# Odd attention of a two-layer mixer: last gate store and first masks ahead of a weight panel, other buffers for the probabilities, output projection waiting bank by bank

## The chip, the cores and the metric

The kernel runs on one core of one Trainium2 chip, as one program written by hand for the engines TensorE (PE in the profile), VectorE (DVE), ScalarE (ACT), GpSimd (POOL) and SyncE (SP), which issues the DMAs. The metric is the device time of one execution in microseconds (us), taken as the median of the runs.

## The reference, cut to what matters

Three layers follow each other over 1024 positions of width 1024: an even layer (windowed attention and a state-space mixer), an odd layer (attention over keys picked by an indexer), and a second block. The change lies in the odd layer, whose core is:

```
q, k, v, gate, qi, ki, wi = split_cols(hn @ w_in, ODD_SPLITS)
q, k = rms_norm(q), rms_norm(k)                  # 8 heads of 128, 2 key/value heads
att = dsa_attention(q, k, v, qi, ki, wi, rel_bias)
return (att * jax.nn.silu(gate)) @ w_out         # h = h + this
```

In `dsa_attention` a query block of 128 positions sees the 256 keys of the highest index score: `logits = q.k / sqrt(Dh) + bias`, everything else is `NEG_INF`, then `softmax` and the product with `v`.

## The kernel before, in words

**Panels.** Every weight matrix comes as panels of at most 128 x 1024 values. SP loads panel i into one of two raw buffers (`sp_panel`, after the low part of panel i-2 has been made from that buffer), ACT rounds it to the high part (`act_panel`, line 297, "w_hi"), POOL subtracts for the low part (`pool_panel`, line 307, "w_lo"), and PE uses three products of high and low parts (line 262). Four panels can be resident.

**The odd layer.** The projection ends with the panels og0 to og7, the gates. For each of them PE makes two halves of 24 matmuls, ACT applies silu into `gev[m % 2]` (line 2382), and SP stores that buffer to DRAM (`gscr`, line 2495, event "og_out" m). Beside it VectorE picks the keys of each block into the mask `MK` (event "keep", lines 2178 to 2187). ACT and POOL convert panel og_m + 4 after gate m; for og7 that is the fourth panel of the output projection.

**The attention** walks over 64 units (n, b), head n and query block b; unit b has 128 (b + 1) keys. All engines write the walk out and pass semaphores, and each engine executes in its own order:

- SP loads one bias strip per head (`load_strip`, line 2480) and one gate per head (`load_gate`, line 2489).
- POOL, `s0` (line 2436): for b of 2 or more, strip plus mask into one of two buffers `bms`.
- PE, `s1`: the products q.k into one of two pairs of PSUM banks, for which the pair has to be free ("od_L" of the unit before the last).
- VectorE, `s1` (line 2235): products plus window into the buffer `pr[i % 3]`, with the row's extreme.
- ACT, `s1` (line 2390): the exponential in place, with the row sums.
- PE, `s2` (line 265): transposes of the probabilities, two units later; ACT (line 2399) or VectorE (line 2250) copies them out.
- After each four blocks `s3`: PE spreads the reciprocal sums and multiplies with the values into bank 3; VectorE scales by sum and gate (lines 2258 and 2261, event "od_g"), ACT takes the high part `MH` (line 443, "od_hi"), POOL the low part `ML` (line 2441, "od_lo"). Q is 0 for blocks 0 to 3 and 1 for blocks 4 to 7.

**The output projection** (`pe_out`, stage "oo") works on t (the first or second 512 positions) and h (the half of the columns). For t = 0, h = 0 it takes three panels one after the other, for each of them the four blocks b in banks 0 to 3, and the fourth panel block by block. VectorE adds the layer's input, which SP has loaded again from DRAM (line 2506), into the result (line 481).

Two buffers share memory with the gates: `gev` lies at H0 + 12 KB and H0 + 16 KB, and `pr` before lies at H0 + 16, 24 and 28 KB. So unit (0, 0) writes over the buffer from which gate 7 is stored, and waits:

```
if (n, b) == (0, 0):
    dve.wait_ge(*at("og_out", 7))
```

The output projection begins after `mixed(t)`, which waits for "od_hi" and "od_lo" of all heads of that t, and for the marks of all four engines at the end of the attention.

Of the kernel before, what the change touches and what calls it, by code (L numbers as in the profile page):

```python
# [17 lines left out]
KB = 1024  # L18
# [1789 lines left out]
class Odd:  # L1808


    def __init__(self, k, E):
        PH, H0, X0 = k.PH0, k.H0, k.X0
        self.XN = E.XN
        self.QT = k.tile(PH, [8, 1024])
        self.KT, self.VN = k.tile(PH + 32 * KB, [2, 1024]), k.tile(PH + 40 * KB, [8, 256])
        self.MK, self.TN = k.tile(PH + 48 * KB, [33 * 128], BF16), k.tile(PH + 48 * KB + 8448, [128])
        O = PH + 48 * KB + 8960
        self.sq = [k.tile(O + 2 * KB * i, [512]) for i in range(2)]
        self.mo = {b: sum(128 * (c + 1) for c in range(2, b)) for b in range(2, 9)}
        self.QI, self.KI = k.tile(H0, [4, 1024]), k.tile(H0 + 16 * KB, [1024])  # L1820
        self.SC = {7: k.tile(H0 + 24 * KB, [1024]), 6: k.tile(H0 + 28 * KB, [896]), 5: k.tile(O + 4 * KB, [768])}

        off = PH + 48 * KB + 2 * self.mo[5] - 768
        for b in (2, 3, 4):
            self.SC[b] = k.tile(off, [128 * (b + 1)])
            off += 512 * (b + 1)
        self.WIT = k.tile(H0 + 24 * KB, [1024])
        self.WI = k.tiny[:, 128:192].rearrange("p (b n) -> p b n", b=8)

        self.by_dve, self.by_act = [6, 4, 3, 2], [7, 5]  # L1830
        self.col = {b: i for i, b in enumerate((6, 4, 3, 2, 7, 5))}
        self.CNT, self.FEW, self.NEED = k.tiny[:, 64:70], k.tiny[:, 70:76], k.tiny[:, 108:114]
        self.TB, self.UB = k.tiny[:, 96:102].bitcast(I32), k.tiny[:, 102:108].bitcast(I32)
        self.ULP, self.BIG = k.tiny[:, 114:116], k.tiny[:, 116:118]
        self.EQ, self.PS = k.tile(H0, [1024]), k.tile(H0 + 4 * KB, [1024])
        at = {6: 0, 4: 1792, 3: 3072, 7: 4096, 5: 6144}
        self.JK = {b: k.tile(H0 + o, [128 * (b + 1)], BF16) for b, o in at.items()}
        self.JK[2] = k.tile(O + 7 * KB, [384], BF16)
        self.rs = k.tile(H0 + 8 * KB, [1024])
        self.gev = [k.tile(H0 + (12 + 4 * i) * KB, [1024]) for i in range(2)]  # L1840
        self.qg, self.ZS = k.tiny[:, 80:81], k.tiny[:, 192:211]
        self.x0 = Ring(k, "od_x0", [0, 1, 2, 3], [("h1", 0, b) for b in range(4, 8)])
        self.x1 = Ring(k, "od_x1", [4, 5, 6, 7], [("h1", 1, b) for b in range(4, 8)])
        self.proj = Ring(k, "od_proj", [0, 1, 2], [("free", "od_x0", "on_t", 0, 4 + i) for i in range(3)])

        self.held = ((3, ("free", "od_x0", "on_t", 0, 7)), (4, ("free", "od_x1", "on_t", 1, 4)))
        self.mis = Ring(k, "od_mis", [5, 6, 7], [("free", "od_x1", "on_t", 1, 5 + i) for i in range(3)])
        self.rel = Ring(k, "od_rel", [k.tile(H0 + 20 * KB + 2 * KB * i, [512]) for i in range(2)])
        self.order = [7, 6, 5, 4, 3, 2]

        self.chain = [("score", b, h) for b in self.order for h in range(8)]
        for i in range(32):
            self.chain += [("count", i, b) for b in self.by_dve + self.by_act] + [("bits", i)]

        done = [min(32, (29 * (u + 1)) // 20) for u in range(32)]
        self.deal = [7 * (b - a) for a, b in zip([0] + done, done)]

        self.norms = [(n, half) for n in (8, 0, 1, 2, 3, 4, 5, 6, 7, 9) for half in range(2)]

        self.bms = [k.tile(H0 + 4 * KB * i, [1024]) for i in range(2)]  # L1860
        self.strips = [k.tile(H0 + o * KB, [1024]) for o in (20, 8)]
        self.pr = [k.tile(H0 + o * KB, [1024]) for o in (16, 24, 28)]
        self.pts = [k.tile(X0, [4, 4, 128]), k.tile(X0 + 8 * KB, [8, 4, 128])]
        self.gts = [k.tile(X0 + (24 + 4 * i) * KB, [1024]) for i in range(2)]
        self.MH, self.ML = k.tile(PH, [8, 1024], F32R), k.tile(X0 + 32 * KB, [8, 1024], F32R)
        self.smr = [k.tiny[:, 128 + 8 * i:136 + 8 * i] for i in range(3)]

        self.sums, self.recs = ([k.tiny[:, o + 4 * i:o + 4 * i + 4] for i in range(2)] for o in (152, 160))
        self.pairs = [4, 6]
        self.ptb = Ring(k, "od_ptb", [0, 1, 2], [("free", "od_proj", "og", *use) for use in ((7, 1), (6, 1), (7, 0))])  # L1870
        self.units = [(n, b) for n in range(8) for b in range(8)]
        self.emb = [k.tile(PH + (48 + 4 * q) * KB, [1024]) for q in range(3)]
# [35 lines left out]
def tensor_odd(k, O):  # L1908
# [143 lines left out]
            s2(*O.units[i - 2])  # L2052
    k.mark("od_att")

    def mixed(t):
        for n in range(8):
            pe.wait_ge(*at("od_hi", n, t))
            pe.wait_ge(*at("od_lo", n, t))
        k.marks(pe, "od_att")

    pieces = [((O.MH, O.ML), 2 * i, 0) for i in range(4)]
    pe_out(k, "oo", lambda t: pieces, lambda t, h, b: [("h2", h, b - 4)] if t else [], mixed,
           lambda part: pe_transposes(k, k.second.x0, "xs", lambda b: k.H[:, b, :], lambda b: [("ln0_y", b)], (0,), range(4 * part, 4 * part + 4)))
    k.mark("odd")


def vector_odd(k, O):
# [152 lines left out]
    def s1(n, b):  # L2220
        nk, i = 128 * (b + 1), 8 * n + b
        p, sm = O.pr[i % 3][:, 0:nk], O.smr[i % 3]
        three = before((n, b), 3)
        if three:
            dve.wait_ge(*at("od_P_turned", *three))
        if b >= 2:
            win = O.bms[b % 2][:, 0:nk]
            dve.wait_ge(*at("od_bm", n, b))
        else:
            win = O.strips[n % 2][:, 1024 - nk:1024]  # L2230
            dve.wait_ge(*at("od_strip", n))
        dve.wait_ge(*at("od_S", n, b))
        if (n, b) == (0, 0):
            dve.wait_ge(*at("og_out", 7))
        V.tensor_tensor_reduce(out=p, in0=k.bank(O.pairs[b % 2], 2)[:, 0:nk], in1=win, scale=-1.0, scalar=3e38,  # L2235
                               op0=ALU.add, op1=ALU.min, accum_out=sm[:, 0:1]).then_inc(*up("od_L", n, b))

# [181 lines left out]
def pool_odd(k, O):  # L2419
    pool, nc, at, up, last = k.pool, k.nc, k.at, k.up, k.last  # L2420
    G = nc.gpsimd
    pool.wait_ge(*at("on_t_ps", 1, 7))
    k.marks(pool, "even")
    G.memset(O.TN, 0.0).then_inc(*up("causal", 0))
    pool.wait_ge(*last("causal"))
    G.affine_select(out=O.TN, in_=O.TN, compare_op=ALU.is_ge, fill=-3e38, base=0, pattern=[[-1, 128]], channel_multiplier=1).then_inc(*up("causal"))
    for name in ("qi0", "qi1", "qi2", "qi3", "ki", "ok0", "ok1", "ov0", "ov1", *(f"oq{m}" for m in range(8)), *(f"og{m}" for m in range(8))):
        pool_panel(k, PANEL_AT[name] + 4)
    def s0(n, b):
        if b >= 2:  # L2430
            nk = 128 * (b + 1)
            pool.wait_ge(*at("od_strip", n))
            pool.wait_ge(*at("keep", 7))
            if (n, b) not in ((0, 2), (0, 3)):
                pool.wait_ge(*at("od_L", *((n, b - 2) if b >= 4 else (n - 1, b + 4))))
            G.tensor_tensor(O.bms[b % 2][:, 0:nk], O.strips[n % 2][:, 1024 - nk:1024], O.MK[:, O.mo[b]:O.mo[b] + nk], ALU.add).then_inc(*up("od_bm", n, b))  # L2436

    def s3(n, Q):
        o = slice(512 * Q, 512 * Q + 512)
        pool.wait_ge(*at("od_hi", n, Q))  # L2440
        G.tensor_tensor(O.ML[:, n, o], O.gts[n % 2][:, o], O.MH[:, n, o].bitcast(F32), ALU.subtract).then_inc(*up("od_lo", n, Q))  # L2441

    s0(*O.units[0])
    for i in range(len(O.units) + 4):
        if i + 1 < len(O.units):
            s0(*O.units[i + 1])
        if i >= 4 and O.units[i - 4][1] % 4 == 3:
            s3(O.units[i - 4][0], O.units[i - 4][1] // 4)
    k.mark("od_att")
    pool_out(k, "oo", "ln0", lambda: k.marks(pool, "od_att"))  # L2450
    k.mark("odd")


def sync_odd(k, O):
# [35 lines left out]

    load_strip(0)
    for m in range(8):
        sp_panel(k, PANEL_AT[f"og{m}"] + 6)
        sp.wait_ge(*at("og", m, 1))
        S.dma_start(d["gscr"][128 * m:128 * m + 128], O.gev[m % 2]).then_inc(*up(f"og_out{m % 2}", by=16, also=[("og_out", m)]))
    sp.wait_ge(*at("og_ps", 7, 1))
    load_gate(0)
    load_strip(1)
    for n, b in O.units:
        if 0 < n < 7 and b == 0:  # L2500
            load_strip(n + 1)
# [1261 lines left out]
```

## Time and profile before

| | |
|---|---|
| median of 3 runs | 2109.1 us (2109.01 to 2120.7) |
| the profiled execution, its own time | 2109.57 us |
| its span in the profile | 2108.3 us |
| mean granted TensorE clock | 0.988 of full |
| PE busy | 2022.3 us, 96% of the span |
| DVE, ACT, POOL busy | 1410.3, 873.4, 653.2 us |

A row of the timeline gives start, duration, engine, line, operation, and output and inputs with the buffer numbers left out; instructions of one kind are merged, and the bracket says how long the engine sat idle before and what released it. The busy share of PE is the share of time in which matmuls are under way. The granted clock is 1.00 at 2.4 GHz and 0.50 at 1.2 GHz; a window that holds a change of level shows a value between.

### The profile page before, as it was taken

How to read it: one execution, taken by the hardware profiler on the slowest of the kernel's cores; microseconds unless marked ns; L12 is line 12 of the kernel's file. 1: busy time of each engine (PE TensorE's matmuls, PEld its weight loads, DVE VectorE, ACT ScalarE, POOL GpSimd, SP SyncE). 2: the span in 40 equal slices, each digit the busy share in tenths (PEclk: the TensorE clock that was granted, in tenths of full speed). 3: DMA queues.
4: the chain of work that ended last, by engine and by line, in shares of the span. 5: the costliest groups of instructions: out<-in, count | busy, mean ns of one | idle time of the engine just before them, and what ended most of it. 6: DMA issues, size and time to landing. Idle time of an engine off the chain costs nothing.

```text
span 2108.3 us, 24436 instructions
## 1 busy us (share of the span) xinstructions
PE 2022.3 (96%) x9260; PEld 1536.7 (73%) x9260; DVE 1410.3 (67%) x2159; ACT 873.4 (41%) x1524; POOL 653.2 (31%) x484
## 2 busy tenths in 40 slices
PE   8999989999999999899999999999999989999997
PEld 6778856787557676566678787888787667778885
DVE  7668676422346889445517699899998756784649
ACT  5333276333445662344412333444224544362431
POOL 3676520552101112345434000000003544235443
PEclk9999999999999999999999999999999999999999
DMA  6422330442401112311043211121133112556322
GB/s 259 134 58 77 109 118 21 170 140 76 135 20 41 41 51 80 100 41 50 21 170 114 86 42 60 32 79 50 60 110 117 64 55 73 193 190 219 110 81 110
DMA packets 72429, 197.91 MB, mean 94 GB/s; under 512 B 11182, under 2 KB 20559, under 8 KB 71800
## 3 DMA queue, kind: packets, MB, share of 16 engines
q1 hardware_dynamic: 72168, 196.35, 27.2%
q8 instruction: 73, 1.20, 0.2%
q14 instruction: 44, 0.36, 0.1%
q10 hardware_dynamic: 144, 0.00, 0.0%
HBM read 152.89 MB, written 46.71 MB: 95 GB/s over the span
## 4 chain that ended last, share of the span: by engine, by line
PE 60%; DVE 16%; ACT 4%; issue 3%; POOL 2%; DMA 2%; SPq 0%; DVEq 0%; ACTq 0%; POOLq 0%
PE psum L262 57%; DVE m L2878 3%; PE psum L265 3%; POOL m L307 1%; DMA m<-in_w 1%; DVE m L2899 1%; DVE m L2111 1%; PE psum L1984 1%; ACT m L297 1%; DVE m L317 1%; DVE m L536 1%; DVE m L452 1%; DVE m L527 1%; DVE m L3070 1%; DVE m L3051 1%
## 5 line engine op out<-in xcount | busy, mean ns | idle before, releaser
L262 PE MATMUL psum<-m,m 128*128 128x512 f32 (+8 forms) x8420 | 1920.8, 393 | 51.9 <-DVE m L2235 10.6
L262 PEld LDWEIGHTS psum<-m,m 128*128 128x128 f32 (+4 forms) x8420 | 1443.0, 187 | 503.3 <-issue 157.6
L307 POOL TENSOR_TENSOR m<-m,m 128x1024 fp32r<-128x1024 f32 (+1 forms) x122 | 309.0, 2537 | 1023.1 <-ACT m L297 1022.7
L297 ACT ACTIVATE m<-m 128x1024 fp32r<-128x1024 f32 (+2 forms) x166 | 173.6, 1049 | 355.0 <-PE psum L262 222.7
L2878 DVE SCALAR_TENSOR_TENSOR m<-m,m,m 128x1024 f32<-128x1024 f32 x240 | 310.2, 1294 | 6.3
L265 PE MATMUL psum<-m,m 128*128 128x128 f32 x784 | 110.5, 277 | 20.3 <-ACT m L2399 5.7
L265 PEld LDWEIGHTS psum<-m,m 128*128 128x128 f32 x784 | 90.5, 142 | 40.8 <-ACT m L1431 10.6
L2111 DVE TENSOR_SCALAR_CACHE_REDUCE m<-m,m 128x896 bf16<-128x896 f32 (+4 forms) x130 | 102.7, 847 | 1.0
L2235 DVE CUSTOM_DVE_ANT_0 m<-psum,m 128x128 f32<-128x128 f32 (+3 forms) x64 | 48.2, 754 | 55.2 <-POOL m L2436 21.5
L2436 POOL TENSOR_TENSOR m<-m,m 128x384 f32<-128x384 f32 (+5 forms) x48 | 72.2, 1525 | 11.3 <-DVE m L2235 11.3
L2341 ACT ACTIVATE m<-m,m 128x1024 bf16<-128x1024 f32 (+1 forms) x62 | 64.1, 1037 | 23.6 <-DVE m L2138 23.6
L2390 ACT ACTIVATE m<-m,m 128x128 f32<-128x128 f32 (+3 forms) x64 | 49.6, 774 | 55.8 <-DVE m L2235 55.8
L2090 DVE SCALAR_TENSOR_TENSOR m<-m,m,m 128x512 f32<-128x512 f32 (+1 forms) x70 | 43.7, 656 | 41.7 <-ACT m L2325 40.1
L317 DVE TENSOR_TENSOR m<-m,m 128x1024 fp32r<-128x1024 f32 (+1 forms) x44 | 52.7, 1198 | 24.6 <-ACT m L297 24.5
L481 DVE TENSOR_TENSOR m<-psum,m 128x512 f32<-128x512 f32 x32 | 21.3, 684 | 66.4 <-PE psum L262 59.9
L443 ACT ACTIVATE m<-m 128x512 fp32r<-128x512 f32 (+1 forms) x38 | 33.5, 883 | 60.6 <-DVE m L2261 52.8
L2325 ACT ACTIVATE m<-psum 128x512 f32<-128x512 f32 (+1 forms) x80 | 38.7, 522 | 42.7 <-PE psum L262 32.1
L465 POOL TENSOR_TENSOR m<-m,m 128x1 f32<-128x1 f32 x23 | 31.5, 1372 | 58.6 <-DVE m L458 58.6
L2441 POOL TENSOR_TENSOR m<-m,m 128x512 fp32r<-128x512 f32 x16 | 20.4, 1274 | 88.4 <-ACT m L443 88.4
L2899 DVE SCALAR_TENSOR_TENSOR m<-m,m,m 128x1024 f32<-128x1024 f32 x36 | 46.2, 1283 | 0.9
L2956 DVE TENSOR_TENSOR m<-m,m 128x1024 f32<-128x1024 f32 x16 | 20.6, 1290 | 38.4 <-ACT m L3233 38.4
L402 DVE SCALAR_TENSOR_TENSOR m<-psum,m,m 128x512 fp32r<-128x512 f32 x32 | 21.6, 743 | 31.3 <-ACT m L391 31.3
(305 smaller groups left out, 1649.4 us busy)
## 6 DMA issues: line engine op xcount, KB each, us to landing
m<-in_w SPq DMA_DIRECT2D x164, 512.0 KB, 3.5
scr_hscr<-m SPq DMA_DIRECT2D x4, 2048.0 KB, 6.6
m<-scr_hscr SPq DMA_DIRECT2D x4, 2048.0 KB, 10.9
scr_turned<-scr_strip SPq DMA_DIRECT2D x8, 575.5 KB, 12.6
m<-in_x SPq DMA_DIRECT2D x4, 1024.0 KB, 7.8
scr_gscr<-m SPq DMA_DIRECT2D x16, 256.0 KB, 4.1
m<-in_x SPq DMA_DIRECT2D x2, 2048.0 KB, 8.4
m<-scr_turned SPq DMA_DIRECT2D x8, 512.0 KB, 3.5
```

Of the source, the lines that this page charges most:

```text
L262: return self.nc.tensor.matmul(out, lhsT, rhs, start=start, stop=stop, skip_group_check=True)
L265: return self.nc.tensor.transpose(out, in_, self.ident[:, :])
L297: k.nc.scalar.activation(k.hi[SLOT[i]][:, 0:kk * n], k.raw[i % 2][:, 0:kk * n], ACT.Copy).then_inc(*k.up("w_hi", i))
L307: k.nc.gpsimd.tensor_tensor(lo, raw, hi.bitcast(F32), ALU.subtract).then_inc(*k.up("w_lo", i))
L317: k.nc.vector.tensor_tensor(lo, raw, hi.bitcast(F32), ALU.subtract).then_inc(*k.up("w_lo", i))
L2111: V.tensor_scalar(O.JK[b], O.SC[b], TF[:, c:c + 1] if i else 0.0, None, how, ALU.add, accum_out=CNT[:, c:c + 1]).then_inc(*up("count", i, b))
L2235: V.tensor_tensor_reduce(out=p, in0=k.bank(O.pairs[b % 2], 2)[:, 0:nk], in1=win, scale=-1.0, scalar=3e38, op0=ALU.add, op1=ALU.min, accum_ ...
L2341: A.activation(O.JK[b], O.SC[b], ACT.Sign, bias=O.TB.bitcast(F32)[:, c:c + 1] if i else 0.0, accum_out=O.CNT[:, c:c + 1]).then_inc(*up("si ...
L2390: A.activation(p, p, ACT.Exp, bias=sm[:, 0:1], scale=-1.0, accum_out=O.sums[b // 4][:, b % 4:b % 4 + 1]).then_inc(*up("od_exp", n, b))
L2436: G.tensor_tensor(O.bms[b % 2][:, 0:nk], O.strips[n % 2][:, 1024 - nk:1024], O.MK[:, O.mo[b]:O.mo[b] + nk], ALU.add).then_inc(*up("od_bm", ...
L2878: V.scalar_tensor_tensor(o, u[:, j:j + 1024], w[:, j:j + 1], o, ALU.mult, ALU.add).then_inc(*up("cv_tap", m, j))
L2899: V.scalar_tensor_tensor(o, x[:, j:j + 1024], cw[:, j:j + 1], o, ALU.mult, ALU.add).then_inc(*up("xb_tap", i, j))
```

## The change

- SP stores the last gate before it loads the weight panel og7 + 6, not behind it; the second strip and the first gate are fetched before that panel too.
- POOL makes the masks of units (0, 2) and (0, 3) before it converts the panel og7 + 4, not behind it.
- The buffers `pr` are at H0 + 24, 28 and 12 KB in place of 16, 24 and 28 KB. Unit (0, 0) waits for no store; unit (0, 2), whose buffer is that of gate 6, waits for "og_out" 6.
- The output projection waits for each bank and each pair of heads where it first uses them, in place of all marks and all heads ahead of its first matmul. SP's own wait for the marks ahead of the reload of the layer's input stays.

```diff
-        self.pr = [k.tile(H0 + o * KB, [1024]) for o in (16, 24, 28)]
+        self.pr = [k.tile(H0 + o * KB, [1024]) for o in (24, 28, 12)]
...
-    def mixed(t):
-        for n in range(8):
+    def free(t, h, b):
+
+        if t:
+            return [("h2", h, b - 4)]
+        if h:
+            return [("od_L", 7, 6 + b // 2)]
+        return [("free", "od_ptb", *O.ptb.holder[b])] if b < 3 else [("od_g", 7, 1)]
+
+    def ready(t, h, i):
+        for n in (2 * i, 2 * i + 1):
             pe.wait_ge(*at("od_hi", n, t))
             pe.wait_ge(*at("od_lo", n, t))
-        k.marks(pe, "od_att")
...
-        if (n, b) == (0, 0):
-            dve.wait_ge(*at("og_out", 7))
+        if (n, b) == (0, 2):
+            dve.wait_ge(*at("og_out", 6))
...
-    for name in ("qi0", "qi1", "qi2", "qi3", "ki", "ok0", "ok1", "ov0", "ov1", *(f"oq{m}" for m in range(8)), *(f"og{m}" for m in range(8))):
+    panels = ["qi0", "qi1", "qi2", "qi3", "ki", "ok0", "ok1", "ov0", "ov1", *(f"oq{m}" for m in range(8)), *(f"og{m}" for m in range(8))]
+    for name in panels[:-1]:
         pool_panel(k, PANEL_AT[name] + 4)
...
-    s0(*O.units[0])
+    for i in range(4):
+        s0(*O.units[i])
+    pool_panel(k, PANEL_AT[panels[-1]] + 4)
     for i in range(len(O.units) + 4):
-        if i + 1 < len(O.units):
+        if 4 <= i + 1 < len(O.units):
             s0(*O.units[i + 1])
...
     for m in range(8):
-        sp_panel(k, PANEL_AT[f"og{m}"] + 6)
+        if m < 7:
+            sp_panel(k, PANEL_AT[f"og{m}"] + 6)
         sp.wait_ge(*at("og", m, 1))
         S.dma_start(d["gscr"][128 * m:128 * m + 128], O.gev[m % 2]).then_inc(*up(f"og_out{m % 2}", by=16, also=[("og_out", m)]))
+    load_strip(1)
     sp.wait_ge(*at("og_ps", 7, 1))
     load_gate(0)
-    load_strip(1)
+    sp_panel(k, PANEL_AT["og7"] + 6)
```

On POOL, where the projection ends and the attention begins, the order before is this (m_62, m_66 and m_70 are the raw, high and low buffers of the panel, m_183 and m_184 the two `bms`, m_185 the strip, m_157 the mask):

```order
L307 TENSOR_TENSOR m_69<-m_63,m_65 128x1024 [waits act_w]
L307 TENSOR_TENSOR m_70<-m_62,m_66 128x1024 [waits act_w]
L2436 TENSOR_TENSOR m_183<-m_185,m_157 128x384 [waits dve_idx,od_strip0]
L2436 TENSOR_TENSOR m_184<-m_185,m_157 128x512
L2436 TENSOR_TENSOR m_183<-m_185,m_157 128x640 [waits dve_od]
```

And with the change, on the same engine at the same place:

```order
L307 TENSOR_TENSOR m_69<-m_63,m_65 128x1024 [waits act_w]
L2445 TENSOR_TENSOR m_183<-m_185,m_157 128x384 [waits dve_idx,od_strip0]
L2445 TENSOR_TENSOR m_184<-m_185,m_157 128x512
L307 TENSOR_TENSOR m_70<-m_62,m_66 128x1024 [waits act_w]
L2445 TENSOR_TENSOR m_183<-m_185,m_157 128x640 [waits dve_od]
```

The two masks of 384 and 512 columns have moved ahead of the last panel's low part; the third mask stays behind it.

On VectorE, the first units of the attention before (m_187 to m_189 are the three `pr`, and out4 is the semaphore of the store of gate 7, out0 that of gate 6; each unit has a second instruction that reads the accumulator):

```order
L2235 ISA m_187,m_59<-psum,m_185 128x128 [waits out4,pe_od,od_strip0]
L2235 ISA m_59 128x1
L2235 ISA m_188,m_59<-psum,m_185 128x256 [waits pe_od]
L2235 ISA m_59 128x1
L2235 ISA m_189,m_59<-psum,m_183 128x384 [waits pe_od,pool_od]
```

And with the change:

```order
L2242 ISA m_187,m_59<-psum,m_185 128x128 [waits pe_od,od_strip0]
L2242 ISA m_59 128x1
L2242 ISA m_188,m_59<-psum,m_185 128x256 [waits pe_od]
L2242 ISA m_59 128x1
L2242 ISA m_189,m_59<-psum,m_183 128x384 [waits out0,pe_od,pool_od]
```

The wait for a store has moved from the first unit to the third, and is for the store of the gate before.

On PE, the first matmuls of the output projection, in one piece of the difference (m_67 and m_71 hold the high and low part of a panel, m_194 and m_195 are `MH` and `ML`):

```order
-L262 MATMUL psum<-m_67,m_194 128x512 [waits pool_od,pe_od,act_od,dve_od,act_w,pool_w]
+L262 MATMUL psum<-m_67,m_194 128x512 [waits act_w,dve_od,pool_w,pool_od]
 L262 MATMUL psum<-m_71,m_194 128x512
 L262 MATMUL psum<-m_67,m_195 128x512
```

The order of the matmuls is the same; the first one waits for earlier events of VectorE and POOL, and for none of ACT, and the nineteenth (block 3, "od_g") has a wait for VectorE of its own.

## Rows read from the trace of the kernel before

**Rows 1.** The page: busy time, share of the span and instructions of each engine.

```profile
PE 2022.3 (96%) x9260; PEld 1536.7 (73%) x9260; DVE 1410.3 (67%) x2159; ACT 873.4 (41%) x1524; POOL 653.2 (31%) x484
```

**Rows 2.** Waits of PE over the run: total, times, longest.

```profile
PE psum L262 <- DVE m L2235: 10.6, 8, 9.5
```

**Rows 3.** Timeline, 855 to 877 us: start us, us, engine, line, operation.

```profile
855.08 0.69 DVE L2187 TENSOR_SCALAR m<-m 128x1024 bf16<-128x1024 f32 x1
...
855.47 11.83 PE L262 MATMUL psum<-m,m 128*128 128x512 f32 x52
...
867.17 1.05 ACT L297 ACTIVATE m<-m 128x1024 fp32r<-128x1024 f32 x1
868.24 1.28 ACT L2390 ACT_TABLE_LOAD   x1
868.30 2.34 POOL L307 TENSOR_TENSOR m<-m,m 128x1024 fp32r<-128x1024 f32 x1 [10.26 <-ACT m L297]
870.59 2.02 POOL L2436 TENSOR_TENSOR m<-m,m 128x384 f32<-128x384 f32 x2
...
871.09 0.42 SPq L2495 DMA_DIRECT2D scr_gscr<-m  x1
...
876.41 0.29 DVE L2235 CUSTOM_DVE_ANT_0 m<-psum,m 128x128 f32<-128x128 f32 x1 [19.32 <-DMA scr_gscr<-m]
...
876.74 0.40 ACT L2390 ACTIVATE m<-m,m 128x128 f32<-128x128 f32 x1 [7.22 <-DVE m L2235]
...
876.76 1.65 PE L262 MATMUL psum<-m,m 128*128 128x384 f32 x2 [9.47 <-DVE m L2235]
```

**Rows 4.** Source line 2495, the store of a gate: issue to landing.

```profile
DMA to landing us min/median/max: 4.9/5.0/5.1
```

**Rows 5.** PE by window: window, length, busy (matmuls), granted clock, DMA share, GB/s.

```profile
871.00:872.00 1.00, 0.00 (x0) 0.79 0.50 57
...
881.00:882.00 1.00, 1.00 (x2) 0.59 0.00 0
```

**Rows 6.** Timeline: POOL's third mask, unit (0, 4).

```profile
879.20 1.40 POOL L2436 TENSOR_TENSOR m<-m,m 128x640 f32<-128x640 f32 x1 [6.59 <-DVE m L2235]
```

**Rows 7.** Timeline, 1052 to 1063 us: end of the attention.

```profile
1052.43 7.05 PE L262 MATMUL psum<-m,m 128*128 128x128 f32 x24
...
1059.59 0.69 DVE L2261 TENSOR_TENSOR m<-psum,m 128x512 f32<-128x512 f32 x1 [5.33 <-PE psum L262]
...
1061.02 1.26 POOL L2441 TENSOR_TENSOR m<-m,m 128x512 fp32r<-128x512 f32 x1 [9.03 <-ACT m L443]
...
1062.67 22.61 PE L262 MATMUL psum<-m,m 128*128 128x512 f32 x90 [3.19 <-POOL m L2441]
```

**Rows 8.** PE in windows of 1 us at the output projection's beginning.

```profile
1062.00:1063.00 1.00, 0.33 (x1) 0.86 0.00 0
...
1066.00:1067.00 1.00, 1.00 (x5) 0.93 1.08 438
```

**Rows 9.** PE in windows of 1 us at another short idle stretch.

```profile
544.00:545.00 1.00, 0.00 (x0) 1.00 0.00 0
...
547.00:548.00 1.00, 1.00 (x5) 0.66 1.00 295
```

**Rows 10.** Timeline: first addition of the layer's input, and the seventh panel's low part.

```profile
1082.54 0.69 DVE L481 TENSOR_TENSOR m<-psum,m 128x512 f32<-128x512 f32 x1 [22.26 <-PE psum L262]
...
1083.24 2.40 POOL L307 TENSOR_TENSOR m<-m,m 128x1024 fp32r<-128x1024 f32 x1 [3.76 <-ACT m L297]
```

**Rows 11.** Source line 2506, two reloads of the layer's input: issue to landing.

```profile
DMA to landing us min/median/max: 7.7/10.8/13.9
```

**Rows 12.** Waits of PE from 1085 to 1200 us.

```profile
PE psum L262 <- issue: 1.8, 1, 1.8
```

**Rows 13.** Timeline of ACT, 1161 to 1163 us: a table load and what follows.

```profile
1161.04 1.28 ACT L3166 ACT_TABLE_LOAD   x1 [2.17 <-DMA scr_hscr<-m]
1162.33 0.69 ACT L3166 ACTIVATE m<-psum,m 128x512 f32<-128x512 f32 x1
```

More of the change, by code:

```diff
@@ L2053, in tensor_odd @@
     k.mark("od_att")
-    def mixed(t):
-        for n in range(8):
+    def free(t, h, b):
[6 more added lines that the diff above has]
+        for n in (2 * i, 2 * i + 1):
             pe.wait_ge(*at("od_hi", n, t))
             pe.wait_ge(*at("od_lo", n, t))
-        k.marks(pe, "od_att")
     pieces = [((O.MH, O.ML), 2 * i, 0) for i in range(4)]
-    pe_out(k, "oo", lambda t: pieces, lambda t, h, b: [("h2", h, b - 4)] if t else [], mixed,
-           lambda part: pe_transposes(k, k.second.x0, "xs", lambda b: k.H[:, b, :], lambda b: [("ln0_y", b)], (0,), range(4 * part, 4 * part + 4)))
+    pe_out(k, "oo", lambda t: pieces, free, lambda t: None,
+           lambda part: pe_transposes(k, k.second.x0, "xs", lambda b: k.H[:, b, :], lambda b: [("ln0_y", b)], (0,), range(4 * part, 4 * part + 4)), 2, ready)
     k.mark("odd")
```

## The prediction

> **What bounds the kernel now.** I began with the page's busy shares: PE has matmuls under way in 96% of the span [rows 1], so only time in which PE stands still or runs at the lower clock can be won; a shorter wait on another engine is worth something only if PE waits behind it. The list of PE's waits came next. Its largest entry, 10.6 us, is a wait for VectorE's line 2235, and one single wait makes 9.5 us of it [rows 2]. The timeline around that wait shows the end of the gate projection and the start of the attention [rows 3], and the same view at the attention's end shows the second place that the change touches [rows 7]. The windows of 1 us then say at which clock PE ran after each [rows 5, 8].
>
> At the first place PE ends its 52 matmuls (48 of gate 7, four of the first two units) at 855.47 + 11.83 = 867.30 us and resumes at 876.76: 9.47 us idle. VectorE had been idle for 19.32 us and started at 876.41, released by the store of the gates. That store was issued at 871.09, behind the load of a weight panel which waited for POOL's low part (868.30 to 870.64), and took about 5 us [rows 3, 4]: 871.09 + 5.1 = 876.2. At the second place PE ends at 1059.48, and the chain VectorE (1059.59), ACT, POOL (until 1062.28) ends before it resumes at 1062.67: 3.19 us idle [rows 7].
>
> **The first wait.** Unit (0, 0) no longer writes into gate 7's buffer, so VectorE starts when PE's first product is there. Before, PE followed 876.76 - 876.41 = 0.35 us after VectorE's start [rows 3]; the same step from 867.3 puts PE's next product at about 867.65. Removed: 9.47 us. New: 0.35 us. Unit (0, 2) waits for the store of gate 6 instead. No row shows that store by itself; stores are issued after ACT's silu of their gate and land after about 5 us [rows 4], and gate 7 alone occupied PE for 48 of the 52 matmuls of an 11.83 us row, so it is long over when the buffer is needed. I cost it at nothing; if the cover were gone, it would be a part of the 5 us.
>
> **The clock behind it.** The granted clock stood at 1.00 until 871.6 us (0.79 in the window from 871) and came back at 881.8 (0.59 in the window from 881) [rows 5]; so from 876.76 to 881.8 PE worked at 1.2 GHz. 5.06 us at half the clock are worth up to 2.5 us where PE sets the pace. In this stretch the engines also hand small units to each other, so the value lies between 0 and 2.5; I take 2.5 here and subtract the new waits singly.
>
> **What is late next: ScalarE's exponential.** The code of ACT is not changed. After gate 7 it copies a panel (867.17 to 868.22), loads the table for the exponential (868.24 to 869.52), and only then can treat unit (0, 0); before, all of this was hidden behind the store, and the exponential came at 876.74, 0.33 us after VectorE's start [rows 3]. Now PE has the product of unit (0, 2) to do, from 867.65, which took 1.65 us at the lower clock [rows 3] and so about 0.8 at the higher, until 868.5; then come the transposes of unit (0, 0), for which the exponential must be done: 869.52 + 0.40 plus a hand-over like the 0.35 above is 870.3. PE waits 1.8 us there. So the bottleneck of the first units becomes ACT's queue, and 0.35 + 1.8 = 2.15 us of the 9.47 remain.
>
> A load of another table followed at once by its activation is in the trace: 1161.04 + 1.28 = 1162.32, and the activation begins at 1162.33 [rows 13]; also, the load at 868.24 begins 0.02 us after the copy before it. The Trainium skill, page "ScalarE: Activation LUTs", section "What ACT_TABLE_LOAD costs", gives 1283 ns for the load and about 1380 ns more of drain for every switch. The first number agrees with the rows, the second is not seen in them. By that rule the exponential would come about 1.4 us later and the sum below would be 1.4 us smaller, an estimate from that page.
>
> **Masks and POOL.** The masks of (0, 2) and (0, 3) take 2.02 us together [rows 3]. POOL sat idle for 10.26 us before 868.30 [rows 3], and the last pass over the mask ends at 855.08 + 0.69 = 855.8 [rows 3], so both fit into the idle stretch and are ready at about 860. They cost nothing, and without this step VectorE would have waited for them until 872.6. The converted panel stays at 868.30 to 870.64, since it waits for ACT. The third mask comes behind it: from 870.64 for 1.40 us [rows 6], thus 8.6 us earlier than its old start at 879.20. POOL thus permits a gain of 8.6 us here plus what slack the mask had; I see it as a bound near the sum, not below it. The panel is the fourth of the output projection, 190 us away.
>
> **SP's queue.** The gate store moves from 871.09 to about 867.7, the strip of head 1 and the gate of head 0 go out behind it, then the panel, whose condition (POOL's low part at 870.64) is not changed. Each issue is a fraction of a microsecond, and the three transfers of half a megabyte land between about 873 and 878; the first gate is needed at the first `s3`, which stands behind eight units' worth of PE's order. Nothing is gained or lost.
>
> **A new spell of low clock.** A fall of the clock can follow rather short idle times: around 544 us PE had one window of 1 us without a matmul, and at 547.7 the clock fell [rows 9]. The spell at the output projection lasted from 1062.72 to 1066.14, 3.42 us [rows 8]. The 2.15 us that remain can bring one like it, at 0 to 1.7 us; I take 0.9.
>
> First place: 9.47 + 2.5 - 2.15 - 0.9 = 8.9 us.
>
> **The second wait.** PE needs for its first matmul the panel (resident), bank 0 (released by VectorE's scaling before the last product), and heads 0 and 1 of the first 512 positions. None of these depends on the last block, whose part ends at 1062.28; that is used only for t = 1, after all of t = 0. Bank 3 is read by VectorE from 1059.59 for 0.69 us, until 1060.28. With the new wait PE comes to it after three blocks of six matmuls. 90 matmuls took 22.61 us [rows 7], 0.25 each, so that is 4.5 us after 1059.5, at 1064: covered by 3.7 us. The whole 3.19 us go, less a hand-over that I put at 0.1.
>
> With the idle stretch the spell from 1062.72 to 1066.14 goes as well: 3.42 x 0.5 = 1.7 us, between 0 (it comes all the same) and 1.7. It is the only idle time of that length near, so I take the whole.
>
> Second place: 3.19 - 0.1 + 1.7 = 4.8 us.
>
> **What follows.** From 1085 to 1200 us PE waits once, 1.8 us, for nothing that the profile shows [rows 12]; the work behind follows PE. SP still waits for all marks ahead of the reload of the layer's input, so relative to the projection the reload becomes 4.8 us later. It lands 7.7 us (first half) and 13.9 us (second) after the issue [rows 11], just behind 1062.3, so by 1070 and 1076.7. VectorE first needs it at 1082.54, now 1077.7: covered by 7 us. The seventh panel's low part ends at 1083.24 + 2.40 = 1085.6 [rows 10]; PE, which uses four panels for the first 22.6 us, comes to the seventh at about 1062.67 + 6 x 5.7 = 1096.9, now 1092: covered by 6 us.
>
> **The sum.** 8.9 + 4.8 = 13.7 us. The profiled execution took 2109.57 us, so 2095.9. The median shown is 2109.1, 0.5 below that execution; I predict 2095.4 us.
>
> **Rivals.**
>
> *The start gains less* (ACT stays behind through several units, a drain behind the table load, POOL's conversion slower beside VectorE). 9.47 + 2.5 - 2.15 - 1.7 - 1.4 = 6.7, and without any value for the old spell 4.2. With 4.8 that is 9.0 to 11.5: 2097.6 to 2100.1. For it speaks that five engines hand over small units there. Against it, that each part alone is small.
>
> *The projection gains nothing*: PE stands again at its first new wait, for instance bank 0 or a panel. Then 8.9 alone, 2100.2. Nothing in the rows supports it.
>
> *More than the sum*: no new spell of low clock (+0.9), and a spell later in the run that falls away because the phases shift, 1.7 us each: 2091 to 2094. To be faster by over 1% (below 2088.0) it would take 21 us; the removable parts, 9.47 + 2.5 + 3.19 + 1.7, are 16.9.
>
> *Slower than before*: the output projection starts while the reload of the input and the weights share the DMA queue, and the addition of the input waits. The price is one microsecond of VectorE, and then of PE through the banks, for each microsecond of landing beyond the 7 us of cover. To lose the 13.7 us too, the first reload would have to land more than 28 us after its issue, where 7.7 and 13.9 are measured.
>
> *The change does not do what it says*: a wait of another name at the same time, such as the strip or a count of stores; 2109. The order shows none.
>
> **How the numbers follow.** The sum as argued, 2093 to 2097.5: 0.67. Start gains less: 0.15. Projection gains nothing: 0.05. More than the sum: 0.09, with 0.03 beyond 1%. Slower or unchanged: 0.04, half of it beyond 1%. A measurement of this kernel can tell about 1% (21 us) from no change, so the gain lies inside "within 1%": faster 0.03, same 0.95, slower 0.02. The range for 8 in 10 goes from 2091.5, where a later spell also falls away, to 2100.5, which takes in the weaker start.
>
> **What would show it.** PE's idle time between gate 7 and unit (0, 2) is 0.3 to 0.5 us, followed by one near 1.8 us that ends with ACT's line 2390 (a few lines lower in the new file). The two first masks stand at 858 to 860 us, ahead of POOL's last panel. The store of gate 7 is issued near 867.7. The clock in the windows from 871 to 881 is 1.00, or has at most one spell of 3.4 us. PE has no idle time between the last product with the values and the projection, and no fall of the clock behind. The prediction fails if PE waits in the first units for POOL's masks, if the clock falls for longer than one spell, or if a new wait appears on weight panels after 1080.

## The result, and the profile after

Twenty runs of each: the changed kernel 2101.9 us median (2095.1 to 2110.3), the kernel before 2113.1 us (2107.6 to 2121.2). The ratio is 0.9941, interval 0.9929 to 0.9954, so 12.5 us less of 2113 (9.7 to 15.0); the two medians differ by 11.2 us. I had forecast 13.7 us less, which lies in that interval, and 2095.4 us, which is wrong: the range ended at 2100.5. The median of the three runs shown of before, 2109.1, was low for this kernel: of the twenty, only two others are as short or shorter, and the comparisons with other runs of it below give 2112.6 (a single run) to 2115.6.

The timeline of the changed kernel, at the beginning of the attention (columns as in [rows 3]):

```profile
859.10 0.69 DVE L2194 TENSOR_SCALAR m<-m 128x1024 bf16<-128x1024 f32 x1
...
859.48 12.81 PE L262 MATMUL psum<-m,m 128*128 128x512 f32 x54
...
862.01 2.04 POOL L2445 TENSOR_TENSOR m<-m,m 128x384 f32<-128x384 f32 x2
...
871.02 0.29 DVE L2242 CUSTOM_DVE_ANT_0 m<-psum,m 128x128 f32<-128x128 f32 x1 [9.92 <-PE psum L262]
871.19 1.05 ACT L297 ACTIVATE m<-m 128x1024 fp32r<-128x1024 f32 x1
...
872.25 1.28 ACT L2397 ACT_TABLE_LOAD   x1
872.31 2.34 POOL L307 TENSOR_TENSOR m<-m,m 128x1024 fp32r<-128x1024 f32 x1 [8.26 <-ACT m L297]
...
873.55 0.40 ACT L2397 ACTIVATE m<-m,m 128x128 f32<-128x128 f32 x1
...
874.10 0.33 PE L265 MATMUL psum<-m,m 128*128 128x128 f32 x1 [1.81 <-ACT m L2397]
874.26 1.02 PE L262 MATMUL psum<-m,m 128*128 128x512 f32 x2
...
875.34 1.25 PE L262 MATMUL psum<-m,m 128*128 128x512 f32 x4
```

These answer to [rows 3]. VectorE starts when PE's product is there, not when a store has landed. The products of unit (0, 2) are merged into PE's row of 54, so the 0.35 us ahead of them is not even shown as idle. The masks (862.01) lie ahead of POOL's panel (872.31). What is late is ScalarE: copy, table load, and 0.02 us behind the load the first exponential; PE stands still for 1.81 us.

At the attention's end, the same view (answers to [rows 7]):

```profile
1046.59 28.76 PE L262 MATMUL psum<-m,m 128*128 128x128 f32 x117
...
1053.75 0.69 DVE L2268 TENSOR_TENSOR m<-psum,m 128x512 f32<-128x512 f32 x1 [5.34 <-PE psum L262]
...
1055.18 1.29 POOL L2450 TENSOR_TENSOR m<-m,m 128x512 fp32r<-128x512 f32 x1 [9.02 <-ACT m L443]
...
1071.88 0.69 DVE L481 TENSOR_TENSOR m<-psum,m 128x512 f32<-128x512 f32 x1 [17.44 <-PE psum L262]
```

The last products with the values and the projection are one row of 117 matmuls: PE doesn't stop while VectorE, ACT and POOL finish the last block. In windows of 1 us (window, length, busy, granted clock, DMA share, GB/s) the clock holds through both places:

```profile
872.00:873.00 1.00, 0.29 (x1) 1.00 0.90 356
873.00:874.00 1.00, 0.00 (x0) 1.00 1.08 242
874.00:875.00 1.00, 0.90 (x3) 1.00 0.96 328
...
1057.00:1058.00 1.00, 1.00 (x6) 1.00 0.46 53
```

**Two stretches as a measure.** An execution differs from the next by several microseconds, so I read two stretches in every trace: from the start of PE's row of gate 7 to VectorE's unit (0, 5) (the row with 128x768), and from there to the first addition of the layer's input (first row of line 481). Unit (0, 5) in the timeline before:

```profile
884.22 0.96 DVE L2235 CUSTOM_DVE_ANT_0 m<-psum,m 128x768 f32<-128x768 f32 x1 [0.70 <-PE psum L262]
```

And after:

```profile
878.38 0.96 DVE L2242 CUSTOM_DVE_ANT_0 m<-psum,m 128x768 f32<-128x768 f32 x1 [0.70 <-PE psum L262]
```

Before, 884.22 - 855.47 = 28.75 us and 1082.54 - 884.22 = 198.32 us (the other two ends are in [rows 3, 10]); after, 878.38 - 859.48 = 18.90 us and 1071.88 - 878.38 = 193.50 us. That is 9.85 + 4.82 = 14.67 us gained. Ahead of gate 7 and behind the addition the code is the same, but gate 7 begins 4.01 us later (859.48, not 855.47), and from the addition to the end of the span it takes 2100.3 - 1071.88 = 1028.4 us, where before it took 2108.3 - 1082.54 = 1025.8. The experiments had to say which of these two differences belong to the change.

### The profile page after: what moved, and what is told of

Same layout as the page of the kernel before. It is cut to its first block, busy times and chain, and to the rows that moved or that the text cites. A ratio compares the mean times of both kernels' runs of the same rounds, so it can differ in the third digit from the quotient of the medians.

```text
span 2100.3 us, 24435 instructions
## 1 busy us (share of the span) xinstructions
PE 2024.0 (96%) x9260; PEld 1538.4 (73%) x9260; DVE 1414.3 (67%) x2159; ACT 873.4 (42%) x1524; POOL 652.2 (31%) x484
## 4 chain that ended last, share of the span: by engine, by line
PE 64%; DVE 14%; ACT 5%; issue 2%; POOL 2%; DMA 1%; SPq 0%; DVEq 0%; ACTq 0%
PE psum L262 60%; PE psum L265 3%; DVE m L2891 2%; POOL m L307 1%; DMA m<-in_w 1%; DVE m L2912 1%; PE psum L1984 1%; DVE m L2118 1%; DVE m L536 1%; ACT m L297 1%; DVE m L452 1%; DVE m L527 1%; DVE m L3083 1%; ACT m L391 1%; DVE m L3064 1%
## 5 line engine op out<-in xcount | busy, mean ns | idle before, releaser
L2450 POOL TENSOR_TENSOR m<-m,m 128x512 fp32r<-128x512 f32 x16 | 20.4, 1275 | 88.3 <-ACT m L443 88.3
```

## The experiments

**Each place alone.** front_only has all of the change but the waits of the projection; end_only has only these, of which this is the core:

```diff
+        return [("free", "od_ptb", *O.ptb.holder[b])] if b < 3 else [("od_g", 7, 1)]
+
+    def ready(t, h, i):
+        for n in (2 * i, 2 * i + 1):
             pe.wait_ge(*at("od_hi", n, t))
             pe.wait_ge(*at("od_lo", n, t))
-        k.marks(pe, "od_att")
```

> Only the beginning of the attention is changed (buffers, first masks, order of SP's issues); the output projection waits as before. Theory A (the two places add, and what is measured elsewhere is the TensorE clock falling at other places by chance): from the start of PE's row of gate 7 to VectorE's unit (0, 5) 18.9 us as in the changed kernel (28.75 before), from there to the first addition of the layer's input 198.3 us as before; time 9.8 us below before, a ratio near 0.9953. Theory B (a shift by the first place brings falls of the clock further down that are there each time, and a part is given back): the same two stretches, but a gain of 5 to 8 us and falls of the clock at about the same later places in each profile of a shifted kernel, near 1220 and 1308 us.

> Only the waits of the output projection are changed; the beginning of the attention is as before. Theory A: from gate 7 to unit (0, 5) 28.75 us, from there to the first addition of the layer's input 193.5 us, 4.8 less than before, of which 3.2 are idle time and 1.6 the clock that does not fall; time 4.8 us below before, ratio near 0.9977. Theory B: the same stretches, but the gain does not show in the time. A further rival: the idle stretch goes and the clock falls all the same, then 195.1 us and a ratio near 0.9985.

front_only: 18.90 and 198.32 us, ratio 0.9951 (0.9934 to 0.9968). end_only: 28.85 and 193.36 us, ratio 0.9981 (0.9968 to 0.9994). The two places add, in the traces to 0.1 us and in time (0.9951 x 0.9981 = 0.9932) within the interval. In end_only the wait and the fall of the clock behind it go together.

**What the order of SP's issues is worth alone.** store_wait_kept:

```diff
-        self.pr = [k.tile(H0 + o * KB, [1024]) for o in (24, 28, 12)]
+        self.pr = [k.tile(H0 + o * KB, [1024]) for o in (16, 24, 28)]
...
-        if (n, b) == (0, 2):
-            dve.wait_ge(*at("og_out", 6))
+        if (n, b) == (0, 0):
+            dve.wait_ge(*at("og_out", 7))
```

> The changed kernel with the old buffers for the probabilities and the old wait of unit (0, 0) for the store of gate 7; the store is still issued ahead of the panel. The store goes out 0.4 us after the silu of gate 7 and takes 5.1 us, so VectorE starts 12.7 + 5.3 = 17 us or a little more after the start of the gate 7 row, 3.5 us earlier than before. Theory A: PE idles 5.7 to 6 us in place of 9.5 and of the changed kernel's 0.4 + 1.8; the exponential no longer has PE wait for its table; from gate 7 to unit (0, 5) 24 to 25.5 us, with a fall of the clock. Rival: if the order of the issues is the whole gain, 19 to 20 us.

21.90 us: less than I expected, more than the rival. The timeline shows why:

```profile
865.81 0.33 SPq L2507 DMA_DIRECT2D scr_gscr<-m  x1
...
868.85 0.29 DVE L2242 CUSTOM_DVE_ANT_0 m<-psum,m 128x128 f32<-128x128 f32 x1 [13.25 <-DMA scr_gscr<-m]
...
869.21 0.91 PE L262 MATMUL psum<-m,m 128*128 128x384 f32 x2 [3.40 <-DVE m L2242]
```

VectorE, which waits for the store, starts 3.0 us after it is issued, so the store took at most that, not 5. In [rows 3, 4], and for gate 6 in this trace, a panel load of the same size goes out 0.4 us ahead of the store; here nothing does, and only the next strip follows 0.4 us behind it. That this is the reason rests on one store, and the view of source line 2507 lists no landing as short (4.9 to 5.1 us). PE waits 3.40 us, the exponential finds its table loaded, and the low clock lasts 3.4 us in place of 10.2. So the order of the issues alone brings 6.85 of the 9.85 us, and the other buffers 3.0.

**The masks.** masks_behind:

```diff
+    pool_panel(k, PANEL_AT[panels[-1]] + 4)
     for i in range(4):
         s0(*O.units[i])
-    pool_panel(k, PANEL_AT[panels[-1]] + 4)
```

> The changed kernel with POOL's first two masks behind the last panel's low part again. POOL's panel ends 15.2 us after the start of the gate 7 row and the mask of (0, 2) takes 0.9 us more, so VectorE has unit (0, 2) at 16.1 and (0, 3) at 17.2 us in place of 12.9 and 16.0. Theory A: from gate 7 to unit (0, 5) 20 to 20.6 us, 1.1 to 1.7 more than the changed kernel, since ScalarE's table load hides the rest. Rival (the moved masks carry the gain): 22 us or more.

21.46 us, 2.56 more than the changed kernel, between my figure and the rival's:

```profile
870.79 2.34 POOL L307 TENSOR_TENSOR m<-m,m 128x1024 fp32r<-128x1024 f32 x1 [10.26 <-ACT m L297]
...
873.08 4.99 POOL L2445 TENSOR_TENSOR m<-m,m 128x384 f32<-128x384 f32 x4
...
874.04 0.56 DVE L2242 CUSTOM_DVE_ANT_0 m<-psum,m 128x384 f32<-128x384 f32 x1 [3.78 <-POOL m L2445]
...
874.66 2.50 PE L262 MATMUL psum<-m,m 128*128 128x512 f32 x4 [0.68 <-DVE m L2242]
```

VectorE waits 3.78 us for the mask, as expected, and PE 0.68 us more; but here the clock falls for 3.4 us (from 874 us on), and the row of four matmuls takes 2.50 us where the changed kernel's takes 1.25 (the row at 875.34 above). I had left that price out.

**The clock as a price of its own.** filled_wait is the kernel before with work in the place of PE's wait:

```diff
     for i in range(len(O.units) + 4):
+        if i == 2:
+            pe.wait_ge(*at("head_ms", 0))
+            for _ in range(10):
+                k.mm(k.bank(3)[:, 0:512], O.QT[:, 0, 0:128], O.KT[:, 0, 0:512], True, True)
```

> The kernel before, with ten extra products of 128 x 512 by TensorE into bank 3 ahead of unit (0, 2), whose result nothing reads: about 9.4 us of matmuls in the 9.47 us in which TensorE stood still. Theory A (the low clock behind the wait is a price of its own, up to 2.5 us): no fall of the clock from 871 to 882 us of the trace before, and from gate 7 to unit (0, 5) 26.2 to 27 us in place of 28.75. Rival (the small units set the pace there, whatever the clock): 28.5 us or more.

26.16 us, with VectorE's first unit at 20.83 us (20.94 before). The wait is as long as ever and the 2.6 us are the clock's. PE's rows:

```profile
861.92 20.41 PE L262 MATMUL psum<-m,m 128*128 128x512 f32 x72
883.10 0.91 PE L262 MATMUL psum<-m,m 128*128 128x384 f32 x2 [0.77 <-DVE m L2239]
```

0.91 us for the products of unit (0, 2), against 1.65 in [rows 3].

**The remaining 1.8 us.** exp_first, on the changed kernel:

```diff
-        act_panel(k, PANEL_AT[f"og{m}"] + 4)
+        if m < 7:
+            act_panel(k, PANEL_AT[f"og{m}"] + 4)
...
         if i < len(O.units):
             s1(*O.units[i])
+        if i == 7:
+            act_panel(k, PANEL_AT["og7"] + 4)
...
-    pool_panel(k, PANEL_AT[panels[-1]] + 4)
     for i in range(len(O.units) + 4):
         if 4 <= i + 1 < len(O.units):
             s0(*O.units[i + 1])
+        if i + 1 == 7:
+            pool_panel(k, PANEL_AT[panels[-1]] + 4)
```

> The changed kernel with the copy of the last panel of the projection moved on ScalarE behind the exponential of unit (0, 7), and its low part on POOL behind the mask of (0, 6). The table load then follows gate 7's silu at once, 1.05 us earlier. Theory A: PE's wait for the exponential of unit (0, 0) shrinks from 1.8 to about 0.75 us, and from gate 7 to unit (0, 5) 17.9 us in place of 18.9; from there to the first addition of the layer's input 193.4 us as before it. In time 1 us below the changed kernel, which a comparison of runs can't tell. Rival (the panel's move costs as much on POOL or SP, since the raw buffer and the next panel come later): the first stretch is 17.9 but the second longer than 193.4, or PE waits for a panel in the projection.

17.96 and 193.40 us, PE's wait 0.9 us: 0.94 us gained, with no cost in the second stretch. In time 0.9925 (0.9908 to 0.9941), beside after_again on the same chip at 0.9930: not told apart. Its two stretches together are the shortest of all traces, but the times do not show it to be faster.

**The same kernels again.**

> The changed kernel once more, nothing edited. Theory A (the level of a single execution is set by where the clock falls in code that the change does not touch): again 18.9 and 193.5 us in the two stretches to 0.2 us, while gate 7 begins at another time than 859.48 us, anywhere from 853 to 863, later where more spells of low clock lie ahead of it; ratio 0.993 to 0.995. Theory B (the change brings the later falls near 1220 and 1308 us): they are there again at those places.

> The kernel before once more, nothing edited. Theory A (where the clock falls outside the two places differs from one execution to the next): 28.75 and 198.3 us in the two stretches, gate 7 beginning anywhere from 853 to 863 us, and falls of the clock beyond 1190 us that need not be those of the first profile. Theory B (the falls near 1220 and 1308 us come with the change): none near 1220 to 1235 or 1308 to 1325 us here either, as in the first profile of the kernel before.

> A second repetition of the kernel before on the same chip. Theory A: again 28.75 and 198.3 us, and a start of gate 7 that differs from the repetition ahead of it by about half of the difference in time spent at the lower clock before it, when TensorE was at work. Theory B: no fall of the clock near 1220 to 1235 or 1308 to 1325 us.

after_again: 18.89 and 193.52 us, ratio 0.9930 (0.9911 to 0.9948). before_again_a: 28.82 and 198.31. before_again_b: 28.91 and 198.32. The two stretches repeat to 0.2 us, the start of gate 7 doesn't. All traces, with the time at the lower clock ahead of gate 7 added up from windows of 1 us:

```
                   gate 7   low clock  1st+2nd   addition  addition  low clock near (us of its own trace)
                   begins   before it  stretch   to 3051   to end    1187    1215-38   1304-22
before             855.47   13.6       227.07    776.0     1025.8    yes     no        no
before_again_a     861.16   27.2       227.13    776.2     1026.3    yes     no        no
before_again_b     856.38   17.0       227.23    776.2     1026.5    yes     no        no
filled_wait        861.92   30.6       224.59    776.7     1025.4    yes     no        no
before_fill_first  859.67   23.8       227.37    776.5     1025.3    no      yes       no
after              859.48   23.8       212.40    778.5     1028.4    no      yes       yes
after_again        862.38   30.6       212.41    777.7     1027.9    no      no        yes
front_only         862.35   27.2       217.22    777.3     1028.0    no      no        yes
end_only           862.21   30.6       222.21    777.8     1027.8    no      yes       yes
store_wait_kept    853.97   10.2       215.25    777.8     1028.5    no      yes       yes
masks_behind       857.95   20.4       214.82    778.5     1028.4    no      yes       no
exp_first          854.52   10.2       211.36    777.9     1028.2    no      yes       yes
after_fill_second  859.69   23.8       212.39    777.7     1026.5    no      no        yes
```

The column "to 3051" ends at VectorE's first instruction of line 3051, which is this row before:

```profile
1858.58 1.23 DVE L3051 TENSOR_TENSOR m<-m,m 128x1024 f32<-128x1024 f32 x1 [0.18 <-ACT m L3310]
```

And this one after:

```profile
1850.43 1.23 DVE L3064 TENSOR_TENSOR m<-m,m 128x1024 f32<-128x1024 f32 x1 [0.18 <-ACT m L3323]
```

First: up to gate 7 the work is the same in all of these, and it takes 853.97 to 862.38 us, in step with the time at the lower clock (20.4 us more of it, 7.4 to 8.4 us later). The 4.01 us by which gate 7 began later in the changed kernel's first trace are this: before_fill_first, whose code up to there is the kernel before, begins it at 859.67 with the same 23.8 us. Most of the spread of the runs goes with it too: of the twenty of the changed kernel, the two at a mean clock of 0.984 took 2108.47 and 2110.26 us and are the slowest, the five at 0.991 took 2095.12 to 2098.3. Theory A holds for that part.

Second: theory A is wrong behind the addition. Leave out the last two experiments (before_fill_first and after_fill_second, below). Seven traces with a part of the change take 1027.8 to 1028.5 us there, four without take 1025.4 to 1026.5. The means are 1028.2 and 1026.0: **2.2 us are given back** in the traces. 14.7 - 2.2 = 12.5 is the measured gain, but the interval of 9.7 to 15.0 us holds 14.7 as well, so the times by themselves do not show the 2.2.

**Where the 2.2 us go.** I followed ScalarE's sixteen activations of its line 3166 (3179 after) through both traces. The changed kernel is 10.66 us ahead at the addition, 10.12 at 1162, still 10.11 at 1401, and 8.32 at 1420 (times of the trace before). The twelfth and thirteenth of them before:

```profile
1401.05 0.69 ACT L3166 ACTIVATE m<-psum,m 128x512 f32<-128x512 f32 x1
...
1420.25 0.69 ACT L3166 ACTIVATE m<-psum,m 128x512 f32<-128x512 f32 x1 [2.61 <-PE psum L262]
```

And after:

```profile
1390.94 0.69 ACT L3179 ACTIVATE m<-psum,m 128x512 f32<-128x512 f32 x1
...
1411.93 0.69 ACT L3179 ACTIVATE m<-psum,m 128x512 f32<-128x512 f32 x1 [2.62 <-PE psum L262]
```

The 0.54 us ahead of 1162 are lost in filled_wait and before_fill_first too, so they are not the change's. Up to 1401 us the falls of the clock near 1220 and 1310 cost nothing in the end, and by 1420, where ScalarE waits for TensorE, they show. I take VectorE's taps (the multiply-adds of the second block's convolution, line 2878) for what sets the pace until about 1400; that is argued, no run shows it. The list of PE's waits in this part, for the kernel before (beside the wait of [rows 12]):

```profile
PE psum L265 <- ACT m L3146: 0.9, 1, 0.9
```

And for the changed kernel:

```profile
PE psum L265 <- ACT m L3159: 2.6, 1, 2.6
PE psum L262 <- issue: 1.8, 1, 1.8
```

Behind the same wait of 1.8 us the clock falls before and does not after; so PE arrives 1.6 us earlier at the next wait, which becomes longer by that much. I took this for the cause of the later falls and tried it from both sides, with products whose results nothing reads: before_fill_first puts seven into the wait of 1.8 us of the kernel before, after_fill_second eight into the wait of 2.6 us of the changed kernel. In both, TensorE's wait for the other engines is also moved behind its wait for a free bank, so that the products can stand between the two.

```diff
-            pe.wait_ge(*at("xs_hi", 1, 7))
-            pe.wait_ge(*at("xs_lo", 1, 7))
...
+        if (what, i, half) == ("gate", 0, 1):
+            for _ in range(7):
+                k.mm(bank, k.XH[:, 0, 0:128], k.XH[:, 0, 0:512], True, True)
+            pe.wait_ge(*at("xs_hi", 1, 7))
+            pe.wait_ge(*at("xs_lo", 1, 7))
```

The second:

```diff
-        pe.wait_ge(*at("xb_silu", i))
+        if i != 9:
+            pe.wait_ge(*at("xb_silu", i))
...
+            if i == 9 and half == 0:
+                for _ in range(8):
+                    k.mm(bank, k.XH[:, 0, 0:128], k.XH[:, 0, 0:512], True, True)
+                pe.wait_ge(*at("xb_silu", i))
```

> The kernel before, with seven extra products of 128 x 512 (about 1.7 us) by TensorE in the 1.78 us in which it waits near 1183 us, at the second block's first panel; nothing reads them. In four traces without a part of the change the clock falls behind this wait (1185 to 1191 us), in seven with a part of it not. Theory B' (the fall there is absorbed, since VectorE sets the pace until about 1400 us, and its absence sends TensorE into a longer wait near 1230 us and to falls near 1230 and 1320 us that are not absorbed): no fall near 1187, TensorE's wait for ScalarE near 1230 us 2.6 us in place of 0.9, and from the first addition of the layer's input to the end of the span 1027.5 to 1028.5 us in place of 1025.4 to 1026.5. Rival (the 2.2 us belong to something else in the change): still 1025.4 to 1026.5 us.

> The changed kernel, with eight extra products of 128 x 512 (1.9 us) by TensorE in its wait of 2.6 us for ScalarE near 1220 us; nothing reads them. Theory B' in its simple form (the long wait brings the falls behind it): no falls near 1220 and 1310 us, and from the first addition of the layer's input to the end 1025.5 to 1026.5 us in place of 1027.8 to 1028.5, so 2 us below the changed kernel, ratio near 0.993 or less. Rival (the fall near 1310 has another origin, as it follows no wait): it is there again and the stretch stays at 1027.8 or more.

before_fill_first: the fall near 1187 is gone, PE's wait is 2.5 us, the clock falls behind it (1238), and yet addition to end takes 1025.3 us: the rival. Only 0.26 us are lost between 1401 and 1420. after_fill_second: no fall near 1220, the one at 1309 is there again, and addition to end takes 1026.5; ratio 0.9931 (0.9908 to 0.9955), not told from the changed kernel. So my account in its simple form falls.

The total of after_fill_second still misleads. At line 3051, more than 400 us behind these places, all thirteen traces stand in two groups that do not overlap: 776.0 to 776.7 us from the addition without the change, 777.3 to 778.5 with a part of it, and after_fill_second is in the second with 777.7. The groups are 1.6 us apart in the mean; this part of what is given back shows in every trace. From there to the end the three kernels with added products (filled_wait and the last two) take 248.7 to 248.8 us and the ten others 249.7 to 250.8, with or without the change. This microsecond lies far behind the filled waits, TensorE's wait for VectorE's line 3017 is 2.3 to 2.4 us in them and 2.7 to 3.3 in the others, and the cause is open. It brings after_fill_second down to 1026.5, and without filled_wait the 2.2 us would be 2.0.

What the traces bear out is a price for each fall, which I read between ScalarE's rows at 1401 and 1420: the one near 1310 alone goes with 1.2 to 1.3 us lost (after_again, front_only, after_fill_second), the one near 1220 alone with 0.26 (before_fill_first, masks_behind), both together with 1.7 to 1.8 (after, end_only, store_wait_kept, exp_first). In masks_behind the rest goes with other falls, at 1492 and 1642. These prices are read off side by side; no run took the fall near 1310 away. Why the fall near 1310 comes in seven of eight traces with a part of the change and in none of five without stays open; it follows no wait that the profile shows:

```profile
1309.00:1310.00 1.00, 1.00 (x7) 1.00 0.00 0
1310.00:1311.00 1.00, 1.00 (x5) 0.84 0.00 0
1311.00:1312.00 1.00, 1.00 (x4) 0.50 0.00 0
```

## Why the prediction was right or wrong

- **The wait for the store** (9.47 us gone, 0.35 and 1.8 new): right. PE's new wait was 1.81 us and for ScalarE's exponential, as worked out.
- **The clock behind it** (up to 2.5, taken whole): right; filled_wait gave 28.75 - 26.16 = 2.59, of which 0.11 is an earlier start.
- **A new spell of low clock** (0.9 set aside): it did not come. With it left out the first place is 9.8 by my terms and 9.85 in the trace; I had 8.9. masks_behind shows that it was a real risk, one further wait away.
- **The drain of the table load** by the Trainium skill, page "ScalarE: Activation LUTs", section "What ACT_TABLE_LOAD costs": not seen. The exponential begins 0.02 us after the load.
- **The masks**: free in their new place, as argued; behind the panel they cost 2.56 us. "VectorE would have waited for them until 872.6" is when both masks end; unit (0, 2) needs the first alone, and in masks_behind VectorE has it 16.09 us after gate 7 begins, which is 871.6 in the trace before.
- **The store's 5 us**: at most 3.0 us in the one case without a panel load right ahead of it. The changed kernel doesn't depend on it.
- **The second wait** (3.19, less 0.1, and 1.7 for the clock): 4.82 measured against 4.8. The reload of the layer's input does not hold up the first addition, which is released by PE.
- **"The work behind follows PE"**: this step failed. I took it from a list of waits that ends at 1200 us. Behind it about 2 us are given back. Two errors partly cancelled here: I set 0.9 us aside at the first place for nothing and counted nothing for what is given back. That 13.7 us came near the measured 12.5 is in part luck.
- **The starting time, and the range**: the step that made the forecast wrong. "The median shown is 2109.1, 0.5 below that execution; I predict 2095.4 us" took three runs as the time of the kernel before, and twenty gave 2113.1. Of the 6.5 us between 2095.4 and 2101.9, 4.0 are this and 2.5 are the change's (13.7 against 11.2 between the medians). The trace had 13.6 us at the lower clock ahead of gate 7, other executions of the same code 10 to 31. With 2113.1 the same sum gives 2099.4, and the range moved by the same 4.0 would be 2095.5 to 2104.5, which holds the measured time. The range was built from the terms alone and held nothing for the spread of runs, though one of the three shown stood 11.6 us above the others.
- **A reading**: the fall that I put at 547.7 us in [rows 9] was at 547.3 (0.66 is about a third of the window at 1.00 and the rest at 0.50). No term of the sum used it.

Of the rivals, "the start gains less" and "the projection gains nothing" did not occur. "More than the sum" had the later falls of the clock vary, but only to the good side; they went to the other.

## What to carry to other kernels

Ahead of a phase change, write down for each engine what is queued there and in which order: here a store behind a panel load, two masks behind another, and an exponential behind a copy, and each was worth 1 to 7 us at one place. An idle stretch of TensorE cost its length and, at both places before, a spell of low clock as well (at the wait of 1.81 us after, none); both are in the windows, and a fill of the wait prices the second alone. When several executions differ by more than the change is worth, forecast the difference, take the time of the kernel before from many runs, and measure stretches between two named rows, which repeated here to 0.2 us for one kernel. Read the experiment's effect close to its place too: the three kernels with added products were 1 us shorter in a stretch hundreds of microseconds behind them.

## What the runs showed of the hardware that I had not expected

- The granted clock falls at places that differ from one execution to the next with the same code: 10.2 to 30.6 us at the lower level within the first 860 us, and with it gate 7 begins up to 8.4 us later. Behind one and the same wait of 1.8 us it fell in four of four traces and, with another part of the kernel changed far ahead of it, in none of eight. Another fall, near 1310 us, follows no wait at all, with TensorE at work in every window around it.
- A fall of the clock on TensorE can stay without effect and be paid much later: those at 1221 and 1310 us of the changed kernel's trace had cost 0.0 us at ScalarE's row of 1390.94 and 1.8 us at that of 1411.93.
- A store of half a megabyte, issued 0.4 us behind a load of the same size, landed after 5.0 us; the one store with nothing issued right ahead of it took at most 3.0 us.
